# Two-layer hybrid trunk on one core: where the mixer's outputs are formed, the last down chunk's buffers, and the LayerNorm affine

## The reference

```
m   = W_o( sig(x Wg_a) * (DilatedAttn(x) W_pa) + sig(x Wg_r) * (Retention(x) W_pr) )
x   = LayerNorm(alpha * x + m)
ple = sigmoid(x W_pg) * (p[i] W_pe)
x   = LayerNorm(alpha * x + ConvGatedMLP(x) + ple)
```

## Time and profile before

| | us |
|---|---|
| median of 3 runs | 1575.04 (1573.39 to 1577.36) |
| the profiled execution, its own time | 1575.79 |
| its span, first to last instruction | 1573.9 |
| TensorE busy | 1536.2 (98%) |
| VectorE busy | 932.6 (59%) |
| ScalarE busy | 753.7 (48%) |
| GpSimd busy | 65.7 (4%) |
| share of the chain that ended last: PE / DVE / issue / ACT / POOL | 93 / 2 / 2 / 2 / 1% |
| granted TensorE clock, mean | 0.996 |

### The profile page before, as it was taken

How to read it: one execution, slowest core, us unless ns; L and a number is a source line. 1 busy time by engine, 2 the same in 40 slices (tenths; PEclk the granted TensorE clock), 3 DMA queues, 4 the chain that set the end, 5 groups by cost and what they waited for, 6 DMA issues and landing times.

```text
span 1573.9 us, 28048 instructions
## 1 busy us (share of the span) xinstructions
PE 1536.2 (98%) x11770; PEld 1486.1 (94%) x11770; DVE 932.6 (59%) x1002; ACT 753.7 (48%) x807; POOL 65.7 (4%) x36
## 2 busy tenths in 40 slices
PE   8999999999999999999999999999999999999997
PEld 7999999999999989999899999998999999999996
DVE  5554654745544587666765646455455445876666
ACT  5354444544543355655544544445445333565552
POOL 0000000000000050000030000000000000400000
PEclk9999999999999999999999999999999999999999
DMA  8535535444365455556545354453553565555651
GB/s 285 186 128 178 171 110 186 138 158 161 108 214 204 164 180 169 206 180 211 170 161 168 123 192 161 135 183 113 165 183 117 180 211 166 170 189 185 196 204 54
DMA packets 231203, 266.09 MB, mean 169 GB/s; under 512 B 4160, under 2 KB 221760, under 8 KB 230592
## 3 DMA queue, kind: packets, MB, share of 16 engines
q1 hardware_dynamic: 230960, 264.44, 50.7%
q10 hardware_dynamic: 144, 0.13, 0.1%
HBM read 263.50 MB, written 1.05 MB: 168 GB/s over the span
## 4 chain that ended last, share of the span: by engine, by line
PE 93%; DVE 2%; issue 2%; ACT 2%; POOL 1%; DMA 0%; POOLq 0%; DVEq 0%; ACTq 0%; SPq 0%
PE bank L1041 26%; PE bank L1042 25%; PE bank L1043 25%; PE acc L1041 3%; PE acc L1042 3%; PE acc L1043 3%; PE acc L1132 1%; PE acc L1141 1%; PE acc L1129 1%; PE acc L1146 1%; PE bank L1146 1%; POOL w_lo L993 1%; DVE w_lo L603 1%; PE acc L1223 0%; DMA X<-x 0%
## 5 line engine op out<-in xcount | busy, mean ns | idle before, releaser
L603 DVE TENSOR_TENSOR w_lo<-raw,w_hi 128x2048 fp32r<-128x2048 f32 x240 | 562.7, 2346 | 412.6 <-ACT w_hi L364 412.2
L1041 PE MATMUL bank<-xT_hi,w_hi 128*128 128x256 f32 x2240 | 637.2, 284 | 4.8 <-DVE w_lo L603 4.8
L1043 PE MATMUL bank<-xT_hi,w_lo 128*128 128x256 f32 x2240 | 633.9, 283 | 0.0
L1042 PE MATMUL bank<-xT_lo,w_hi 128*128 128x256 f32 x2240 | 633.9, 283 | 0.0
L364 ACT ACTIVATE w_hi<-raw 128x2048 fp32r<-128x2048 f32 x243 | 463.9, 1911 | 161.5 <-PE bank L1043 94.0
L1041 PEld LDWEIGHTS bank<-xT_hi,w_hi 128*128 128x128 f32 x2240 | 429.8, 192 | 7.0 <-DVE w_lo L603 4.6
L1042 PEld LDWEIGHTS bank<-xT_lo,w_hi 128*128 128x128 f32 x2240 | 429.9, 192 | 1.6
L1043 PEld LDWEIGHTS bank<-xT_hi,w_lo 128*128 128x128 f32 x2240 | 429.8, 192 | 0.0
L1041 PE MATMUL bank<-w_hi,xT_hi 128*128 128x256 f32 x768 | 219.6, 286 | 11.3 <-issue 8.2
L1042 PE MATMUL bank<-w_lo,xT_hi 128*128 128x256 f32 x768 | 217.5, 283 | 2.0 <-issue 2.0
L1043 PE MATMUL bank<-w_hi,xT_lo 128*128 128x256 f32 x768 | 217.2, 283 | 0.0
(11 more groups left out here) (169 smaller groups left out, 1507.6 us busy)
## 6 DMA issues: line engine op xcount, KB each, us to landing
raw<-w_in SPq DMA_DIRECT2D x135, 1024.0 KB, 5.0
raw<-w_up SPq DMA_DIRECT2D x44, 1024.0 KB, 5.1
raw<-w_down SPq DMA_DIRECT2D x22, 1024.0 KB, 5.0
raw<-w_ret_proj SPq DMA_DIRECT2D x16, 1024.0 KB, 5.1
raw<-w_attn_proj SPq DMA_DIRECT2D x8, 1024.0 KB, 5.2
raw<-w_out SPq DMA_DIRECT2D x8, 1024.0 KB, 5.0
raw<-w_ple_gate SPq DMA_DIRECT2D x8, 1024.0 KB, 5.1
scratch<-ln_rows SPq DMA_DIRECT2D x4, 1024.0 KB, 7.0
```

What stands on the lines that cost most here:

```text
L603: nc.vector.tensor_tensor(slot_lo[s], raw[:, raw_slot(c), :], slot_hi[s].bitcast(F32), ALU.subtract).then_inc(lo_ready, 1)
L1041: mm(dst, st_hi, mv_hi, start=start, stop=False)
L1042: mm(dst, st_hi, mv_lo, start=False, stop=False)
L1043: return mm(dst, st_lo, mv_hi, start=False, stop=stop)
```

## The change

1. Mixer outputs. `attend` and the transposes of ret_y leave the end of the iteration; a new `finish` does them on TensorE behind chunk 0 of the next iteration, or of the merge. ScalarE's and VectorE's parts of it stand behind their split of chunk 3. Both heads' outputs go to acc[0] and acc[1].
2. Last down chunk. Its raw data get a place in scratch (`last_raw`), loaded ahead of the MLP loop; `last_hi` and `last_lo` lie in the memory of ret_hi, and are made behind the last steady turn, which is written out behind a loop of 7. The chunk leaves the ring, so a layer has 122 ring chunks and not 123. The residual moves from ahead of the MLP loop to ahead of `last_lo`.
3. LayerNorm. `rows` on VectorE replaces `normalised`, `x_transposed` and GpSimd's `update_x`: in halves of 512, (Y - mean) * g, then * 1/std + b into X. TensorE transposes X by halves. GpSimd's w_lo of the next layer's chunk 1 goes to VectorE; that of ple's gate chunk 0 stays. The store goes out in four pieces of 256 KB.

```diff
-C_LAYER = C_MLP + 3 * NF
+C_LAYER = C_MLP + 3 * NF - 1
...
+        last_hi, last_lo = ret[:, 0, :], ret[:, 1, :]
+        last_raw = view(6144, (CE,))
...
+        def slot(l, c):
+
+            return (c + l * C_LAYER) % RING
...
+                sp.wait_ge(chunk_done, L0 + C_PLE + RING)
+                sp.dma_start(last_raw.rearrange("p (k n) -> p k n", k=2), part(w_down, l, 2 * NF - 2, 2, 0, D))\
+                  .then_inc(last_loaded, 16)
...
+                for h in range(2):
+                    v = slice(h * 512, (h + 1) * 512)
+                    sp.wait_ge(x_rows, 4 * (2 * DEPTH - 1) + 2 * t + h + 1)
+                    sp.dma_start(out[t * P:(t + 1) * P, v], X[:, t, v]).then_inc(stored, 16)
...
@@ scalar @@
-            def x_high(m, t, l=None, w=0):
...
+            def x_high(m, t):
+
                 for h in range(2):
-                    if l is not None:
-                        act.wait_ge(xT_f_ready[h], (m - 1) * TT + t + 1)
+                    act.wait_ge(lnT_done, m * 4 + 2 * t + h + 1)
                     nc.scalar.activation(xT_hi[:, 4 * h:4 * h + 4, t * P:(t + 1) * P],
                                          acc[2 * t + h][:, :].rearrange("p (k t) -> p k t", k=4),
                                          ACT.Copy).then_inc(xT_hi_ready, 1)
+
+            def finish(l, j, done):
+
+                act.wait_ge(ret_yT_done, done)
...
+                ins.then_inc(ret_affine, 1)
+                for a in range(2):
+                    act.wait_ge(pv_done, done * 2 - 1 + a)
+                    nc.scalar.activation(attn_hi[:, bass.ds(j * 2 + a, 1), :],
+                                         acc[a][:, 0:SEQ].rearrange("p (a b) -> p a b", a=1),
+                                         ACT.Copy).then_inc(attn_hi_ready, 1)
+                act.wait_ge(ret_gated, done)
+                nc.scalar.activation(ret_hi[:, bass.ds(j * 4, 4), :], ret_t, ACT.Copy).then_inc(ret_hi_ready, 1)
...
+                    if c == 1 and not first:
+                        finish(l, value(j - 1), it)
...
+                act.wait_ge(last_loaded, 16 * (l + 1))
+                nc.scalar.activation(last_hi, last_raw, ACT.Copy).then_inc(last_hi_ready, 1)
...
@@ vector @@
-            def normalised(n, t):
-
+            def rows(n, t):
+
+                dve.wait_ge(rows_in, 16 * (n + 1))
+                for h in range(2):
+                    v = (slice(None), t, slice(h * 512, (h + 1) * 512))
+                    nc.vector.scalar_tensor_tensor(out=Y[v], in0=Y[v], scalar=mv_ln[:, t, 0:1],
+                                                   in1=ln_gb[:, 0, h * 512:(h + 1) * 512],
+                                                   op0=ALU.subtract, op1=ALU.mult).then_inc(ln_by_g, 1)
                 dve.wait_ge(ln_rstd, n * TT + t + 1)
-                nc.vector.tensor_scalar(Y[:, t, :], Y[:, t, :], mv_ln[:, t, 0:1], rs_ln[:, t:t + 1],
-                                        ALU.subtract, ALU.mult).then_inc(ln_y, 1)
-
-            def x_transposed(l, m, w, t):
-
-                g0, b0 = PC_LN + 2 * w * KT, PC_LN + (2 * w + 1) * KT
-                dve.wait_ge(lnT_done, m * 4 + 2 * t + 1)
-                for k in range(4):
-                    o = acc[2 * t][:, k * P:(k + 1) * P]
-                    ins = nc.vector.tensor_scalar(o, o, feat[:, l, g0 + k:g0 + k + 1],
-                                                  feat[:, l, b0 + k:b0 + k + 1], ALU.mult, ALU.add)
-                ins.then_inc(xT_f_ready[0], 1)
+                for h in range(2):
+                    v = (slice(None), t, slice(h * 512, (h + 1) * 512))
+                    dve.wait_ge(ln_by_g, n * 4 + 2 * t + h + 1)
+                    nc.vector.scalar_tensor_tensor(out=X[v], in0=Y[v], scalar=rs_ln[:, t:t + 1],
+                                                   in1=ln_gb[:, 1, h * 512:(h + 1) * 512],
+                                                   op0=ALU.mult, op1=ALU.add).then_inc(x_rows, 1)
 
...
+            def finish(j, done):
+
+                dve.wait_ge(ret_affine, done + 1)
+                nc.vector.tensor_tensor(ret_t, ret_t, silu, ALU.mult).then_inc(ret_gated, 1)
+                for a in range(2):
+                    dve.wait_ge(attn_hi_ready, done * 2 - 1 + a)
+                    nc.vector.tensor_tensor(attn_lo[:, bass.ds(j * 2 + a, 1), :],
+                                            acc[a][:, 0:SEQ].rearrange("p (a b) -> p a b", a=1),
+                                            attn_hi[:, bass.ds(j * 2 + a, 1), :].bitcast(F32),
+                                            ALU.subtract).then_inc(attn_lo_ready, 1)
+                dve.wait_ge(ret_hi_ready, done + 1)
+                nc.vector.tensor_tensor(ret_lo[:, bass.ds(j * 4, 4), :], ret_t,
+                                        ret_hi[:, bass.ds(j * 4, 4), :].bitcast(F32),
+                                        ALU.subtract).then_inc(ret_lo_ready, 1)
...
-                for t in range(TT):
-                    dve.wait_ge(x_updated[t], n2 + 1)
+                def steady(g, i):
...
+                with dve.Fori(0, NF - 4) as i:
+                    steady(dve.snap(L0 + C_MLP + i * 3), i)
+                steady(L0 + C_MLP + (NF - 4) * 3, NF - 4)
                 dve.wait_ge(ple_ready, (l + 1) * NJ)
                 nc.vector.scalar_tensor_tensor(out=X[:, :, :], in0=X[:, :, :], scalar=ALPHA, in1=ple,
                                                op0=ALU.mult, op1=ALU.add).then_inc(residual_ready, 1)
-                with dve.Fori(0, NF - 3) as i:
...
+                dve.wait_ge(last_hi_ready, l + 1)
+                nc.vector.tensor_tensor(last_lo, last_raw, last_hi.bitcast(F32), ALU.subtract)\
+                  .then_inc(last_lo_ready, 1)
...
-                to_lo(l, L0, TAIL + 6)
...
-                    normalised(n, 0)
-                    x_transposed(l, n + 1, 1, 0)
+                    rows(n, 0)
+                    to_lo(l + 1, g, 1)
                     x_low(n + 1, 0)
+                    to_lo(l + 1, g, 2)
                     summed(n, 2)
                     summed(n, 3)
                     mean_and_variance(n, 1)
-                    normalised(n, 1)
-                    to_lo(l + 1, g, 2, behind=True)
-                    x_transposed(l, n + 1, 1, 1)
+                    rows(n, 1)
                     x_low(n + 1, 1)
...
@@ gpsimd @@
-            def update_x(n):
-                pool.wait_ge(rows_in, 16 * (n + 1))
-                pool.wait_ge(xT_lo_ready, 4 * (n + 2))
-                for t in range(TT):
-                    nc.gpsimd.tensor_tensor(X[:, t, :], Y[:, t, :], ln_gb[:, 0, :], ALU.mult).then_inc(x_by_g[t], 1)
-                for t in range(TT):
-                    pool.wait_ge(x_by_g[t], n + 1)
-                    nc.gpsimd.tensor_tensor(X[:, t, :], X[:, t, :], ln_gb[:, 1, :], ALU.add).then_inc(x_updated[t], 1)
...
@@ tensor @@
-            def transpose_y(n, t):
-                pe.wait_ge(ln_y, n * TT + t + 1)
-                transpose_tile(Y, n + 1, t)
...
+            def transpose_half(m, t, h):
+                for k in range(4 * h, 4 * h + 4):
+                    ins = nc.tensor.transpose(acc[2 * t + h][:, (k % 4) * P:(k % 4 + 1) * P],
+                                              X[:, t, k * P:(k + 1) * P], ident)
+                ins.then_inc(lnT_done, 1)
+
+            def transpose_x(n, t):
+                for h in range(2):
+                    pe.wait_ge(x_rows, n * 4 + 2 * t + h + 1)
+                    transpose_half(n + 1, t, h)
+
+            def finish(done):
+
+                pe.wait_ge(ret_y_ready, done)
+                pe.wait_ge(probT_copied, done * 2)
+                for t in range(TT):
+                    for k in range(4):
+                        ins = nc.tensor.transpose(acc[2 + k // 2][:, (k % 2) * SEQ + t * P:(k % 2) * SEQ + (t + 1) * P],
+                                                  ret_y[:, t, k * P:(k + 1) * P], ident)
+                ins.then_inc(ret_yT_done, 1)
+                for a in range(2):
+                    for i in range(NG):
+                        mm(acc[a][:, 0:SEQ], att_v[:, i, 0, a * P:(a + 1) * P], probT[:, a, i, 0:SEQ],
+                           start=(i == 0), stop=False)
+                        ins = mm(acc[a][:, P:SEQ], att_v[:, i, 1, a * P:(a + 1) * P], probT[:, a, i, SEQ:384],
+                                 start=False, stop=(i == NG - 1))
+                    ins.then_inc(pv_done, 1)
...
+                    if c == 0:
+                        finish(it)
...
-                attend(0, bank[1])
-                attend(1, acc[0])
...
+                finish((l + 1) * NJ)
...
+                                if c is None:
+                                    pe.wait_ge(last_lo_ready, l + 1)
```

More of the change, by code:

```diff
@@ L132, in view @@
             return v
-        slot_hi = [w_hi[:, s, :] for s in range(RING)] + [attn[:, 0, :]]
-        slot_lo = [w_lo[:, s, :] for s in range(RING)] + [attn[:, 1, :]]
-        attn_hi = attn[:, 0, :].rearrange("p (h t) -> p h t", h=HEADS)
```

(23 more changed lines are left out.)

312 lines of the change are left out of this document (120 added, 192 removed).

## The result

| | before | after |
|---|---|---|
| median of the runs, us | 1575.06 (1573.39 to 1577.36) | 1558.91 (1558.40 to 1560.72) |
| profiled execution, its own time, and its span | 1575.79, 1573.9 | 1560.72, 1558.9 |
| TensorE busy | 1536.2 | 1534.0 |
| granted TensorE clock, mean | 0.996 | 0.998 |

The ratio is 0.9900, with the interval 0.9888 to 0.9912: 16.1 us less, where 7.5 were forecast and 1561 was the lower end of the range. The sign is right, the size is half.

The account below looks back on a forecast made before the run. TensorE, busy 1536.2 of 1573.9 us, was taken as the bound, leaving 37.7 us of starving to win. Terms -4.0 - 8.0 + 3.8 + 1.2 - 0.5 = -7.5 us gave 1567.5 against the median; range 1561 to 1573.

Parts of the forecast that it names:

- terms of the MLP: MLP, both layers: the early residual gains 4.0 us in all and the last down chunk's own buffers 8.0.
- Mixer outputs, forecast 0: Mixer: moving attention and transposes behind the next chunk 0 makes no wait and wins nothing; cost 0.
- the "issue" gap is tied to the branch, and the branch stays: Mixer loop's back branches: the four first gaps, 6.4 us together, stay unchanged.
- Rival C: Mixer's back branches: the sequencer gets further ahead, all four first gaps go, 6.4 us, giving 1561.1; chance 0.13.
- Rival B: Mixer's back branches: look-ahead counted in instructions, gaps grow, 4 x 2.9 = 11.6 us, giving 1579.1; chance 0.07.
- Residual, -2.0 a layer: First MLP turn: with the residual behind the last steady turn, TensorE waits about 0.1 us instead of 2.08.
- Last down chunk, -4.0 a layer: MLP's end: own buffers shorten TensorE's wait by 2.3 us and save 1.7 us of low clock.
- Rival A: Last down chunk: VectorE's lag grows to over 3 us, the wait stays; price 8.0 us, 1575.5; chance 0.13.
- LayerNorm 1, +1.9 a layer: LayerNorm 1: later rows and tile 1 waiting for GpSimd's w_lo lose 1.9 us a layer, 3.8 in all.
- LayerNorm 2, +1.2: LayerNorm 2, layer 0: waits for rows let 2.8 of 4.0 us won arrive, a loss of 1.2.
- End, -0.5: End, layer 1: halves add 0.1 us, the smaller last store takes off 0.6; gain 0.5.
- rival D: LayerNorms: waits of 1.6 to 2 us cost the clock at three places, 5.1 us, 1572.6; chance 0.07.

Follow-up runs that it names:

- e1: Before, with TensorE's code moved by 96 instructions that wait for nothing: 1571.19 us (ratio 0.9972).
- e5: After, with TensorE's code moved by 124 instructions, made of small matmuls in time in which it waits for x anyway: 1551.20 us.
- e8: After, with the residual put back ahead of the MLP loop: 1564.42 us (ratio 0.9929).
- e7: After, with the last down chunk's split back at the end of ScalarE's and VectorE's queues, its own buffers kept: 1561.99 us (ratio 0.9912).
- e3: Before, with only the mixer outputs moved behind the next chunk 0 on all three engines: 1572.10 us (ratio 0.9976).
- e4: Before, with only the LayerNorm by rows in halves, no GpSimd update of X, and the store in four: 1577.45 us (ratio 1.001).
- e10: After, with the LayerNorm rows in whole instructions of 1024 instead of halves: 1565.64 us (ratio 0.9931).
- e2: After, with 132 satisfied waits (66 instructions) at the start of TensorE's program: 1575.93 us (ratio 0.9997).
- e11: After, with GpSimd's last w_lo (ple's gate chunk 0) given to VectorE behind tile 0's rows: 1565.92 us (ratio 0.9936).
- e12: After, with TensorE's mixer loop written out and GpSimd's last w_lo given to VectorE: 1555.48 us (ratio 0.9869).

## Why the prediction was half right

The terms of the MLP came out as forecast, and the forecast won only half of the time because two others were wrong: the mixer's, put at 0 (it was -3.0), and those of the LayerNorms, put at +5.0 (they were +1.4). 1558.9 lies below the stated range.

1. **Mixer outputs, forecast 0: failed.** The step that failed is "the 'issue' gap is tied to the branch, and the branch stays". The branch stayed and four of the eight gaps went; e1 and e5 keep it and have none. The gap is tied to the place of the code. In before a return cost two gaps (1.82 and 0.76 us at the first return), in after one. This is before's second gap, then after's two returns of layer 0:

```profile
219.71 0.39 PE L1041 MATMUL bank<-w_hi,xT_hi 128*128 128x256 f32 x1 [0.76 <-issue]
```

```profile
211.85 0.38 PE L1013 MATMUL bank<-w_hi,xT_hi 128*128 128x256 f32 x1 [1.66 <-issue]
...
314.55 0.38 PE L1013 MATMUL bank<-w_hi,xT_hi 128*128 128x256 f32 x1 [2.03 <-issue]
```

   By the count above, the block of the branch's target now ends some 48 matmuls behind it instead of 15. The four second gaps, 3.7 us, are gone; the four first grew from 6.4 to 7.1, and one of them cost the clock:

```profile
1084.69 0.38 PE L1013 MATMUL bank<-w_hi,xT_hi 128*128 128x256 f32 x1 [1.96 <-issue]
```

```profile
1084.70:1089.10 4.40, 4.40 (x24) 4.40 (x25) 2.29 (x1) 1.12 (x1) 0.00 (x0) 0.61 0.37 124
```

   Rival C was right that gaps can close, and wrong on what closes them: it made that depend on the order of the work. Its price of 6.4 us also left out the second gaps. Rival B, with its look-ahead counted in instructions, is refuted by e5: same order, no gap.
2. **Residual, -2.0 a layer: right.** The first turn's wait is gone, e8 brings it back whole, and VectorE is in time at the chunk behind its new place.
3. **Last down chunk, -4.0 a layer: right, a little small.** It measured -4.1 and -4.2. The wait went whole (2.75 instead of 2.3), and the clock is full behind it. What I had not seen is that the chunk's own memory does more than half of it without the move: e7's stretch is only 1.5 us a layer longer than after's. And there is luck in the size: I took the 1.7 us of low clock as sure, and in layer 1 of e1, e3 and e4 the same wait left the clock full. Rival A is refuted.
4. **LayerNorm 1, +1.9 a layer: right sign, twice too big** (0.9). I had 1/std at 1.52 us beside halves; it takes 0.98. And I let tile 1's first pair wait for the end of GpSimd's w_lo (566.76 in after), but it ran beside it, 1.72 us instead of 1.41:

```profile
562.15 4.61 POOL L979 TENSOR_TENSOR w_lo<-raw,w_hi 128x2048 fp32r<-128x2048 f32 x1 [3.86 <-DVE w_lo L596]
...
566.25 1.72 DVE L634 SCALAR_TENSOR_TENSOR scratch<-scratch,stat 128x512 f32<-128x512 f32 x2
```

   The Trainium skill's rule (SBUF — State Buffer, SBUF: two separate sides) is that the two engines hold the shared port pair in turn, each for its whole instruction. GpSimd getting in between two halves agrees with 0.98 instead of 1.53. But by that turn the second half would wait as well, and the second pair would start at about 2.05; the two halves take 1.41 us beside 1/std, as two of 0.69 do alone, and the second pair starts at 1.32. There the trace disagrees. I had named the rule and kept 1.79, and both are too long.
5. **LayerNorm 2, +1.2: wrong sign** (-0.4). Tile 1's wait is 1.24 us and not 2, the halves again. That is less than what went: the w_lo of 3.77 us, and TensorE's waits of 0.66 and 0.62 us at 789.47 and 809.28 in before.
6. **End, -0.5: right sign** (-0.9). The four stores land 2.0 us after issue, where two of 512 KB took 2.6.
7. **The clock, rival D:** at the LayerNorms it didn't fall in after, where the waits stay under 1.3 us. It fell in e10 behind 2.42. So it can happen there, but no wait of that size is left in after.

Of the versions run, after with TensorE's mixer loop written out (1550.79) and after with its code moved (1551.20) beat both kernels; the first has no return to pay for, wherever its code lies. It takes 25.0 us off the 1575.76 measured beside it, of which 8.1 to 8.8 are the loop's (against after's median, and against what after takes off the before beside it).

## What to carry to other kernels

An idle time with no releaser behind a long loop's back branch was instruction fetch here: look at the packets of the instruction queue first. If they are more than the program is long, move the code or write the loop out, and don't credit or blame the order of work. A change that adds or drops instructions ahead of such a loop changes its time on its own, so an A/B of two kernels needs their packet counts side by side. Memory of its own for a late chunk can be worth as much as an earlier place in the queue; and where one engine's small result stands between two passes over a row, two half passes hid here what one whole pass didn't.

## What the hardware showed that I had not expected

- A TensorE loop of 6.4 blocks of code runs without any fetch at its returns at some places in the program (50 packets in all) and fetches nine blocks a return at others (86). Without the fetches the two mixers together take 12.1 us less than in before, and 9.6 less than in the profiled run of after (7.7 by the medians); at one return of e2 the two gaps were 2.06 and 1.97 us.
- The same 1/std on GpSimd takes 0.55 us alone, 0.98 beside two halves and 1.53 beside a whole instruction of VectorE.
- Whether the clock falls behind an idle of about 2 us is not settled by its length. It stayed full behind 2.08 in both layers of before, behind 2.03 in after (314.55) and behind 2.75 in layer 1 of e3 and e4. It fell behind 1.96 (after, 1084.69), 1.83 (e3, 313.94), 2.08 (e8, 611.75) and 2.42 (e10), and once at a wait of 1.64 (e11, 574.52) that left it full in e11's layer 1 and in both layers of e12. A fall costs 1.3 to 1.7 us. What decides stays open, and one trace with or without a fall says little on an edit.
